# Even mixer ending in token layout, gate weights from broadcast rows, and a new order of first loads and tail in a diffusion trunk step

## What is computed

```
def even_mixer(h, w_in, lb, hgrn_g, gate_bias, mlstm_g, w_out, s_hgrn, s_c, s_n, s_m):
    qa, fa_f, fa_b, ia, ga, qb, kb, vb, ob, gates = split_cols(h @ w_in, EVEN_SPLITS)
    ...
    oa = rms_norm(oa_f + oa_b, hgrn_g) * jax.nn.silu(heads(ga, HA))          # HGRN2, 4 heads of 128
    ...
    hb = rms_norm(hb_f + hb_b, mlstm_g) * jax.nn.sigmoid(heads(ob, HB))      # mLSTM, 4 heads of 128
    mix = jnp.concatenate([oa.reshape(B, T, -1), hb.reshape(B, T, -1)], axis=-1)
    return mix @ w_out, new

# one direction of the mLSTM
        m_t = jnp.maximum(w_state, jnp.max(w_in, axis=2))
        qk = jnp.einsum('bthk,bshk->btsh', qc, kc) * jnp.exp(w_in - m_t[:, :, None, :])
        s_state = jnp.exp(w_state - m_t)
        num = jnp.einsum('btsh,bshv->bthv', qk, vc) + s_state[..., None] * jnp.einsum('bthk,bhkv->bthv', qc, C)
        den = jnp.sum(qk, axis=2) + s_state * jnp.einsum('bthk,bhk->bth', qc, n)
        h = num / jnp.maximum(jnp.abs(den), jnp.exp(-m_t))[..., None]
```

## Time and profile before

| | us |
|---|---|
| median of 3 runs | 1253.37 (1251.84 to 1255.16) |
| the profiled execution, whole | 1250.76 |
| its span | 1248.9 |
| PE busy in the span | 1154.1 (92%) |
| DVE, ACT, POOL busy | 444.4, 430.8, 541.0 |
| mean granted TensorE clock | 0.956 of full speed |
| moved by DMA | 163.84 MB, 131 GB/s |

### The profile page before, as it was taken

One profiled execution on the slowest core, in us unless ns is written; L12 is line 12 of the kernel. 1 busy time (PEld: TensorE's weight loads), 2 busy tenths in 40 slices (PEclk: granted clock), 3 DMA queues, 4 the chain that ended last, 5 costly groups with the idle time before them and its releaser, 6 DMA issues.

```text
span 1248.9 us, 17436 instructions
## 1 busy us (share of the span) xinstructions
PE 1154.1 (92%) x7238; PEld 1047.4 (84%) x7238; DVE 444.4 (36%) x822; ACT 430.8 (34%) x658; POOL 541.0 (43%) x414
## 2 busy tenths in 40 slices
PE   5699998999988999999999989778998999999997
PEld 3399898977767999999999869565597999999996
DVE  4523899215766311111111230428655101111112
ACT  0442422452343423322222242447615333323222
POOL 0344588330015364554455524113043565565662
PEclk9599999989999999999999979889998999999998
DMA  9743323345234666655566642042025444434331
GB/s 311 252 127 104 101 68 102 118 136 189 82 85 138 180 188 185 187 169 170 164 202 184 173 158 68 17 119 68 1 68 135 111 125 135 121 105 117 116 117 51
DMA packets 242940, 163.84 MB, mean 131 GB/s; under 512 B 20214, under 2 KB 241453, under 8 KB 242862
## 3 DMA queue, kind: packets, MB, share of 16 engines
q1 hardware_dynamic: 214880, 135.74, 37.5%
q10 hardware_dynamic: 27982, 26.99, 6.9%
HBM read 159.81 MB, written 2.90 MB: 130 GB/s over the span
## 4 chain that ended last, share of the span: by engine, by line
PE 74%; DVE 12%; ACT 5%; DMA 3%; POOL 3%; issue 2%; ACTq 0%; SPq 0%; DVEq 0%
PE banks L410 19%; PE banks L412 18%; PE banks L411 18%; POOL w_lo L1014 3%; PE banks L484 3%; ACT w_hi L1038 2%; DVE ht L1467 1%; PE banks L450 1%; PE banks L452 1%; PE banks L451 1%; DMA raw<-in_ada_w 1%; DVE h_lo L1458 1%; DVE Qd L1635 1%; DMA raw<-in_w_in_even 1%; DVE Kd L1635 1%
## 5 line engine op out<-in xcount | busy, mean ns | idle before, releaser
L1014 POOL TENSOR_TENSOR w_lo<-raw,w_hi 128x512 fp32r<-128x512 f32 (+2 forms) x410 | 540.8, 1349 | 685.3 <-ACT w_hi L1038 685.3
L410 PE MATMUL banks<-h_hi,w_hi 128*128 128x384 f32 x1152 | 394.6, 343 | 24.4 <-DVE h_lo L1458 16.7
L411 PE MATMUL banks<-h_lo,w_hi 128*128 128x384 f32 x1152 | 388.8, 338 | 0.0
L412 PE MATMUL banks<-h_hi,w_lo 128*128 128x384 f32 x1152 | 388.7, 337 | 0.0
L1038 ACT ACTIVATE w_hi<-raw 128x2048 fp32r<-128x2048 f32 (+4 forms) x115 | 193.4, 1682 | 206.3 <-PE banks L412 157.8
L410 PEld LDWEIGHTS banks<-h_hi,w_hi 128*128 128x128 f32 x1152 | 218.5, 190 | 37.9 <-issue 30.7
L411 PEld LDWEIGHTS banks<-h_lo,w_hi 128*128 128x128 f32 x1152 | 218.7, 190 | 0.7
L412 PEld LDWEIGHTS banks<-h_hi,w_lo 128*128 128x128 f32 x1152 | 218.3, 190 | 0.6
L1510 DVE TENSOR_TENSOR uf<-sa,banks 128x384 f32<-128x384 f32 x44 | 24.4, 554 | 330.2 <-PE banks L412 324.2
L410 PE MATMUL banks<-u_hi,w_hi 128*128 128x384 f32 x352 | 118.8, 338 | 0.9 <-POOL w_lo L1014 0.9
L412 PE MATMUL banks<-u_hi,w_lo 128*128 128x384 f32 x352 | 117.7, 334 | 0.0
(11 more groups left out here) (348 smaller groups left out, 1288.2 us busy)
## 6 DMA issues: line engine op xcount, KB each, us to landing
raw<-in_ffn_w SPq DMA_DIRECT2D x88, 512.0 KB, 5.2
raw<-in_ada_w SPq DMA_DIRECT2D x28, 1024.0 KB, 5.9
raw<-in_ffn_w SPq DMA_DIRECT2D x32, 704.0 KB, 4.6
vada_raw<-in_ada_w ACTq DMA_DIRECT2D x20, 1024.0 KB, 6.7
raw<-in_w_in_even SPq DMA_DIRECT2D x18, 1024.0 KB, 5.2
raw<-in_w_out_even SPq DMA_DIRECT2D x4, 1024.0 KB, 5.7
raw<-in_w_in_odd SPq DMA_DIRECT2D x3, 1024.0 KB, 7.3
raw<-in_w_in_odd SPq DMA_DIRECT2D x8, 256.0 KB, 4.4
```

The costliest lines, as they stand in the source:

```text
L410: pe.matmul(out, s_hi, m_hi, start=first and j == 0, stop=False)
L411: pe.matmul(out, s_hi, m_lo, start=False, stop=False)
L412: mm = pe.matmul(out, s_lo, m_hi, start=False, stop=last and j == len(terms) - 1)
L1014: ins = pool.tensor_tensor(w_lo[s % SPLIT][:, at:to], raw[u % RAW][:, at:to], w_hi[s % SPLIT][:, at:to].bitcast(F32), ALU.subtract)
```

## The change

1. **Order of the units.** `in0_0` is loaded after three pairs of `ada_w` instead of four, and the pair of place "norm0" moves from behind `in0_0` to between `in0_13` and `in0_14`. PE runs that pair ahead of `in0_14`, DVE takes it after the level loop. DVE's work on the HGRN lower bounds moves behind the first norm; ACT splits the second unit after the first norm rather than ahead of it; the loads of S0, C0 and m0 go to ACT's step j = 7.
2. **Norm.** ACT loads one table set that has both Ln and Exp, in place of the dummy Ln.
3. **Token layout.** `ga` (units 8, 9) and `ob` (16, 17) come out in token layout. `vb` gets a column of ones and C0 a column with n0, so that numerator and normaliser come out of one matmul of 129 columns; `hg_o` comes out in token layout.
4. **mLSTM weights.** ACT writes the rows of m to DRAM at j = 14 (four DMAs) and reads them back spread over 128 partitions at j = 15 (two DMAs, 1.5 and 0.5 MB). POOL adds the masks, eight tiles of 128 x 384 (`mask_weights`, new L1030), four behind the `w_lo` of `in0_16` and four behind that of `in0_17`. PE turns m to columns at j = 15. The selector matmuls of `decays` go.
5. **The mixer's loop.** For each j PE has `states` and `inner`; DVE's `finish` has one add of 387 columns, maximum, maximum and reciprocal of three columns, and three scalings of 128. Sums of squares are reduced on DVE and the norms' Ln and Exp taken on 12 or 3 columns. Each head is turned back to features by three PE transposes (`turn_head`); ACT writes `h_hi` and DVE `h_lo` from that bank. The output projection starts when the banks of the loop have been read.
6. **Tail.** PE turns X to tokens behind each tile of the last FFN product (`turn_y`), DVE multiplies by the gain (`take_y`), the squares are summed by matmuls of one column, Ln and Exp work on 3 columns, and three output DMAs of 512 KB are left.

```diff
-    ada("start")
+    ada("start", range(0, 3))
     add("in0", 1, DT, 256)
-    ada("norm0")
+    ada("start", range(3, 4))
     add("in0", 6, DT, 256, 1)
     add("gates", 1, DT, 16)
-    add("in0", 11, DT, 256, 7)
+    add("in0", 7, DT, 256, 7)
+    ada("norm0")
+    add("in0", 4, DT, 256, 14)
...
             for j in range(6, 18):
-                if j in (6, 7, 14, 15):
+                if j == 14:
+                    modulation("norm0")
+                if not 10 <= j < 14:
                     for c in range(NCH):
                         tokens(("in0v", j, c), number[("in0", j)], 0, 256, c)
...
+            def states(j):
+                bk = mix.fill(pe, ("X", j))
+                if j < 2 * H:
+                    h, d = j // 2, j % 2
+                    for c in (1, 2):
+                        mm = pe.matmul(bk[:, (c - 1) * (P + 1):c * (P + 1)], qm[:, h, c * P:(c + 1) * P], C0[:, d, h, :],
+                                       start=c == 1, stop=c == 2, skip_group_check=True)
+                if j:
+                    pe.wait_ge(S["k_in_ready"], j)
+                    mm = pe.matmul(bk[:, 2 * (P + 1):3 * (P + 1)], k_in[:, (j - 1) % 2, :], vb[:, 0, (j - 1) // 2, :],
+                                   start=j == 2 * H, stop=True, skip_group_check=True)
+                mm.then_inc(mix.done, 1)
+            def inner(j):
+                h, d = j // 2, j % 2
+                bk = mix.fill(pe, ("num", j))
+                pe.wait_ge(S["A_ready"], j + 1)
+                blocks = ((1, 2), (0, 0), (1, 1), (2, 2)) if d == 0 else ((0, 0), (1, 1), (2, 2), (2, 1))
+                for i, (s, t) in enumerate(blocks):
+                    mm = pe.matmul(bk[:, t * (P + 1):(t + 1) * (P + 1)], Aw[:, j % 2, i * P:(i + 1) * P], vb[:, s, h, :],
+                                   start=i == 0, stop=i == 3, skip_group_check=True)
+                mm.then_inc(mix.done, 1)
...
+            qk(0)
+            states(0)
+            for j in range(2 * H):
+                if j % 2 and j < 2 * H - 1:
+                    qk(j // 2 + 1)
+                states(j + 1)
+                inner(j)
+                modulation("mlstm", ada_pairs("mlstm")[j:j + 1])
+                for i in TURN_HEADS.get(j, ()):
+                    turn_head(i)
...
+            def mask_weights(first, end):
+                for j in range(first, end):
+                    pool.wait_ge(S["weights_in"], 32)
...
+                    pool.tensor_tensor(e, e, big, ALU.add).then_inc(S["weights_masked"], 1)
...
             def norm(n, base):
-                act.activation(table_col[:, :], eps_col[:, :], ACT.Ln)
+                act.preload_act_table_set("natural_log_exp_and_others")
...
+                elif j == 15:
+                    act.wait_ge(S["qi_ready"], 2)
+                    act.wait_ge(S["m_rows_out"], 64)
+                    act.dma_start(E_all, rows[0:3072].partition_broadcast(P)).then_inc(S["weights_in"], 16)
+                    act.dma_start(E67[:].rearrange("p j t -> p (j t)"), rows[3072:4096].partition_broadcast(P))\
+                        .then_inc(S["weights_in"], 16)
...
+            def finish(j):
+                h, d = j // 2, j % 2
+                bk = mix.filled(dve, ("num", j))
...
+                dve.tensor_tensor(n2, all3, state_part[:, j % 2], ALU.add).then_inc(mix.read(("num", j)), 1)
+                mix.was_read(dve, ("num", j))
+                step(dve.scalar_tensor_tensor(dn, n2[:, :, P], -1.0, n2[:, :, P], ALU.mult, ALU.max))
+                step(dve.tensor_tensor(dn, dn, em[:, :, d, h], ALU.max))
+                step(dve.reciprocal(dn, dn))
+                for c in range(NCH):
+                    if d == 0:
+                        ins = dve.tensor_scalar(hm[:, c, h, :], n2[:, c, 0:P], dn[:, c:c + 1], None, ALU.mult)
+                    else:
+                        ins = dve.scalar_tensor_tensor(hm[:, c, h, :], n2[:, c, 0:P], dn[:, c:c + 1], hm[:, c, h, :],
+                                                       ALU.mult, ALU.add)
...
+                    if l == 1 and m:
+                        turn_y(m - 1)
```

More of the change, by code:

```diff
@@ L1471, in norm @@
                         low(m - 1)
[L1472 removed]
+                    if place is not None:
+                        modulation(place, ada_pairs(place)[m:m + 1])
                 low(DT - 1)
```

549 lines of the change are left out of this document (293 added, 256 removed).

## The result

The changed kernel takes 1212.72 us (median of four, 1211.46 to 1215.29) where the kernel before takes 1254.17 beside it: a ratio of 0.9681, with a 95% interval of 0.9662 to 0.9701. The forecast was 1211, range 1196 to 1226.

What follows compares the result with a forecast made beforehand. PE was taken as full in the projection's last stretch and the mixer, with start and tail open. Terms -7.3 + 0.6 + 11.0 - 39.1 - 2.8 - 4.5 = -42.1 from 1253.4 gave 1211 us, range 1196 to 1226.

Steps and rivals of the forecast that it cites:

- The mixer: Last `hg_o` to first product of `out0`: 55.2 us against 94.25, -39.1, with DVE the bound by 8 us; range 49 to 74.
- the lead-in of 4.1: In the mixer's sum of DVE work: 4.1 us on DVE until the first weights.
- Rival A: Mixer: PE's work runs at the low clock and PE bounds again; 1230, or 1220 for half of it; chance 0.22.
- The start: Up to the second unit of the input projection: earlier first product, then a PE wait of 5.0; -7.3, range -5 to -10.
- What would show it: List of expected signs, among them first product of `in0_0` at 44 to 46 and mixer about 55 us.
- token units 8 and 9: Input projection: same columns through PE in more instructions, moved loads covered by POOL's slack; +0.6, range 0 to +3.
- The end of the projection: Last stretch of the input projection, PE without idle time: pair, two waits, token units, transposes; +11.0, range +5 to +14.
- the transposes of m: End of the input projection: six transposes, twelve short PE instructions, +0.7.
- Rival B: The two new waits at the projection's end do not show and DVE has no gaps; 1198, chance 0.19.
- rival C: Before `in0_17`: the 2 MB read-back lands late and stalls POOL's queue and PE; slower than before; chance 0.02.
- Norms 1 and 3: One table load of 1.28 us and the dummy leave each norm's path: 1.4 each, -2.8.
- Rival D: Norms: a table switch costs more than its row, 2.66 us with drain by the skill page; 1207, chance 0.02.
- The tail: After the last FFN product: transposes and scalings leave the end, 16.3 becomes 9.8, transposes between products add +2.0; -4.5, range -3 to -6.

Runs made afterwards that it cites:

- the doubled matmuls: Changed kernel with the four `inner` matmuls made twice in each step of the mixer, the second overwriting the same sums: median 1212.30 us.
- the add: Changed kernel with one more DVE add of 387 columns, into an unread scratch, in each of the mixer's eight steps: median 1217.01 us against 1214.68.
- light kernels: Changed kernel and kernel before, each with POOL computing only the first 512 columns of each unit's `w_lo` from the third on: medians 1176.96 and 1228.38 us.
- the five later runs: The changed kernel run again without edit, five more times: median 1214.68 us (1212.78 to 1217.85).
- three edits: Against the changed kernel: pair norm0 moved into the mixer, all masks behind `w_lo` of `in0_17`, S0/C0/m0 loads on SP; singly 1211.06, 1213.29, 1208.80, together 1199.61 us.

## Why the prediction was right, and where it was not

**The mixer (-39.1; measured -39.6 and -37.9 in the two profiles)** was right in its size, and its reason is borne out in part. DVE is busy for 42.61 of 54.69 us, where the sum had 49.2 of work. Of that sum, the lead-in of 4.1 is mostly time in which DVE waits, and the operations were a little cheaper (`finish` 1.8 in place of 2.1, a head's scaling 0.84 in place of 1.0); against that, DVE's gaps, the lead-in and the last head's chain through ACT, DVE and PE among them, were 12 us, where the sum had 4.1 and 6. The errors cancel nearly, and that is luck. The sum had DVE as the bound by 8 us over PE; measured, PE is busy for 44.00 us and DVE for 42.61, so neither is full, and the time is that of the chain between them. That PE alone is not the bound is shown by the doubled matmuls; that DVE's work is on the path is shown in part by the add. Rival A is refuted: the granted clock was 0.89, and more work on PE did not lengthen the mixer.

**The start (-7.3; -9.1)** was right in each of its steps: first product at 43.55 (44.7 forecast), first unit's end at 54.8 (55.5), second unit from 59.21 (60.5) after a wait of 4.46 (5.0). "What would show it" asked for a first product at 44 to 46 and a wait of 5, so both came a little sooner than that.

**The step that failed is the one on the levels**, "token units 8 and 9, +0.6; range 0 to +3". The prediction took the moved loads of S0, C0 and m0 as covered ("the three loads that go to j = 7 have POOL's slack beside them"), and counted the start's gain as if it passed through the levels unchanged. In the profile of before, DVE was busy for 79.38 of the 82.90 us ahead of level 7. That is an engine with no slack, whose operations take twice as long when POOL is at work. With the loads moved to SP, the 6.1 us of the levels come back; with the pair's place in the queue of units alone changed, 2.1. The two are not independent: together they give back 4.3. In each case the sum of DVE's operations moves the same way. A range of 0 to +3 did not hold it.

**The end of the projection (+11.0; +13.4)** had every wait in its place and nearly in its size: pair 1.93 for 2.1, waits 2.91 and 2.44 for 3.0 and 3.0. Mis-sized were the other two terms. The light kernels, both at a clock of 1.00 without a gap, have 51.8 and 47.5 us for this stretch; less the pair's 1.93, the token units and the transposes of m cost 2.3 us there, where the prediction had 1.3. And PE is busy for 6.4 us more in the change than in its light kernel (58.16 against 51.75) and for 2.7 more in the kernel before than in its own (50.22 against 47.48): a loss to the clock of 3.7 more than before, where the prediction had 0.8 for each wait. Rival B, that these waits do not show and that DVE has no gaps, is refuted, and rival C too: the spread rows landed in 8.1 us.

**Norms 1 and 3 (-2.8; -0.2 at each).** The table load went from the path, as the rows of before and after show, but POOL's `w_lo` set when DVE's first pair of `ht` ended. The light kernels give the 1.38 us that the term had, at each of the two. The step that failed is taking DVE's start as the norm's pace; the prediction gave no work that takes its place.

Rival D, a drain beyond the table load's own row, is not borne out by these runs: in the changed kernel Ln begins at 366.82, 0.02 us behind the end of the load at 366.80. The Trainium skill, page "ScalarE: Activation LUTs", section "What ACT_TABLE_LOAD costs", has 2.66 us for a switch with its drain; the trace shows 1.28, and the drain is not to be seen in it. Nor does it show in the time: taking the load from between Ln and Exp at the last norm gave 1.28.

**The tail (-4.5 with the transposes; about -4.8)** was right: 9.66 us for 9.8 forecast, and some 1.8 us more ahead of it (2.0 forecast). No run has the transposes of X alone, so that these 1.8 are theirs is argued from the window.

In sum the forecast of 1211 was right for the right main reason, and nearer than its parts deserve. By the parts it was 6.8 us too hopeful (35.3 against 42.1), and the median did not show that because the profiled run of before was 2.6 to 3.4 us faster than the medians and that of the change 2.6 slower than that of its four. Against the five later runs (1214.68) the forecast is 3.7 too low.

## What to carry to other kernels

A gain at the start of a chain is kept only if the stretches behind it keep their length. Look for the stretch where another engine has no idle time and a third can slow it down (here DVE and POOL): every edit that shifts one against the other, even three DMA issues, can have a price of microseconds, and the place to test is one run with the other engine's work cut. Compare such a run stretch by stretch, since its whole time moves for other reasons too. Waits of the matmul engine are best removed together, since one that stays can keep the clock low behind it: three edits that gave 10.9 us singly gave 15.1 together.

## What the runs showed of the hardware

- DVE's operation of 128 x 768 took 0.94 us with POOL idle and 2.01 beside POOL's subtraction, and POOL's four tiles of 128 x 512 took 5.0 alone and 7.1 to 11.6 beside DVE. Both sides pay. The same 49 operations of DVE took 61.5 to 68.9 us in sum, by how the two queues met, and 48.7 and 49.8 with POOL's work cut to a quarter.
- A table load between two dependent activations cost 1.28 us, its own row and no more: with it Exp began 1.89 us after Ln, without it 0.61.
- With PE's work in the mixer raised by 64 instructions, the mixer did not get longer (54.4 us against 55.1 and 56.7) and its granted clock rose from 0.89 to 0.97.
- Behind a wait of PE of 3.12 us the granted clock fell to 0.50; behind one of 3.38 at the same place in another kernel it stayed at 1.00.
- Two DMAs that spread 16 KB of DRAM over 128 partitions as 2 MB landed in 7.2 and 8.1 us after their issue, while weights came in beside them.
